# Attention values held high and low side by side: two matmuls for each value tile in place of three

## The reference

```python
kv = (rmsnorm(h_kv, kv_norm_g) @ w_ukv).reshape(B, S, MLA_HEADS, MLA_NOPE + MLA_V)   # 8 heads, 64 + 64
k_nope, v = kv[..., :MLA_NOPE], kv[..., MLA_NOPE:]
s = (jnp.einsum('bqhd,bkhd->bhqk', qn, k_nope) + jnp.einsum('bqhr,bkr->bhqk', qp, k_pe))
p = jax.nn.softmax(s.astype(jnp.float32) * scale, axis=-1).astype(v.dtype)
o = jnp.einsum('bhqk,bkhd->bqhd', p, v)
```

## Time and profile before

| what | value |
|---|---|
| median of 3 runs | 1538.49 us (1537.92 to 1539.16) |
| profiled execution, its own time | 1535.2 us |
| its span, first to last instruction | 1533.4 us |
| TensorE busy | 1472.2 us (96%) |
| VectorE busy | 780.0 us (51%) |
| ScalarE busy | 685.5 us (45%) |
| GpSimd busy | 659.9 us (43%) |
| TensorE clock granted, mean | 0.988 of full |

### The profile page before, as it was taken

One profiled execution on the slowest core, in us unless ns is written; L12 is line 12 of the kernel. 1 busy time (PEld: TensorE's weight loads), 2 busy tenths in 40 slices (PEclk: granted clock), 3 DMA queues, 4 the chain that ended last, 5 costly groups with the idle time before them and its releaser, 6 DMA issues.

```text
span 1533.4 us, 19452 instructions
## 1 busy us (share of the span) xinstructions
PE 1472.2 (96%) x6870; PEld 1201.8 (78%) x6870; DVE 780.0 (51%) x1186; ACT 685.5 (45%) x1082; POOL 659.9 (43%) x317
## 2 busy tenths in 40 slices
PE   8998899999999999999999888999999999999996
PEld 6676679888878888888878666898888888888884
DVE  7648768533464430345164776792525445014534
ACT  5556636444344431344355664463534444124432
POOL 4343226743344444343545321485443443534350
PEclk9999999999999999999999998999999999999998
DMA  5320124521233233322323101254122322422231
GB/s 199 97 82 15 42 68 139 165 83 42 83 97 107 77 118 97 96 82 82 127 83 102 50 29 55 83 169 134 41 83 82 109 82 85 124 97 84 81 96 56
DMA packets 39033, 138.76 MB, mean 90 GB/s; under 512 B 4848, under 2 KB 5104, under 8 KB 38704
## 3 DMA queue, kind: packets, MB, share of 16 engines
q1 hardware_dynamic: 37584, 134.24, 28.0%
q10 hardware_dynamic: 1376, 3.52, 0.7%
HBM read 135.64 MB, written 2.10 MB: 90 GB/s over the span
## 4 chain that ended last, share of the span: by engine, by line
PE 75%; issue 10%; DVE 8%; POOL 4%; ACT 2%; DMA 1%; SPq 0%; POOLq 0%; DVEq 0%; ACTq 0%
PE ps L1322 24%; PE ps L1324 24%; PE ps L1323 24%; POOL w_lo L340 4%; PE ps L1474 1%; DVE small L1008 1%; DMA x<-xT_d 1%; DVE h_lo L1034 0%; DVE small L1038 0%; PE ps L1497 0%; DVE arena L1034 0%; DVE work L855 0%; DVE work L1111 0%; PE ps L1332 0%; DVE work L1020 0%
## 5 line engine op out<-in xcount | busy, mean ns | idle before, releaser
L340 POOL TENSOR_TENSOR w_lo<-raw,w_hi 128x1024 fp32r<-128x1024 f32 x248 | 604.6, 2456 | 718.6 <-ACT w_hi L435 718.3
L1322 PE MATMUL ps<-h_hi,w_hi 128*128 128x512 f32 (+1 forms) x1040 | 408.2, 392 | 10.2 <-POOL w_lo L340 4.7
L1324 PE MATMUL ps<-h_hi,w_lo 128*128 128x512 f32 (+1 forms) x1040 | 404.4, 389 | 0.0
L1323 PE MATMUL ps<-h_lo,w_hi 128*128 128x512 f32 (+1 forms) x1040 | 404.1, 389 | 0.0
L435 ACT ACTIVATE w_hi<-raw 128x1024 fp32r<-128x1024 f32 x248 | 256.1, 1054 | 326.1 <-PE ps L1324 325.5
L1322 PE MATMUL ps<-arena,w_hi 128*128 128x512 f32 (+2 forms) x656 | 244.0, 372 | 0.9 <-DVE arena L990 0.9
L1324 PE MATMUL ps<-arena,w_lo 128*128 128x512 f32 (+2 forms) x656 | 242.0, 369 | 0.0
L1323 PE MATMUL ps<-arena,w_hi 128*128 128x512 f32 (+2 forms) x656 | 241.8, 369 | 0.0
L1322 PEld LDWEIGHTS ps<-h_hi,w_hi 128*128 128x128 f32 x1040 | 196.1, 189 | 53.8 <-issue 9.3
L1323 PEld LDWEIGHTS ps<-h_lo,w_hi 128*128 128x128 f32 x1040 | 196.2, 189 | 40.6 <-issue 1.0
L1324 PEld LDWEIGHTS ps<-h_hi,w_lo 128*128 128x128 f32 x1040 | 195.9, 188 | 40.5
(11 more groups left out here) (171 smaller groups left out, 1813.1 us busy)
## 6 DMA issues: line engine op xcount, KB each, us to landing
raw<-blocks_d SPq DMA_DIRECT2D x248, 512.0 KB, 3.6
x<-xT_d SPq DMA_DIRECT2D x4, 512.0 KB, 7.7
work<-memT_d ACTq DMA_DIRECT2D x2, 1024.0 KB, 5.2
outT_d<-work SPq DMA_DIRECT2D x8, 256.0 KB, 2.1
work<-ln_d ACTq DMA_DIRECT2D x2, 512.0 KB, 3.4
par<-par_d ACTq DMA_DIRECT2D x2, 113.5 KB, 5.7
work<-pos_d ACTq DMA_DIRECT2D x1, 128.0 KB, 3.7
mix_g<-par_d SPq DMA_DIRECT2D x1, 4.0 KB, 1.6
```

The costliest lines, as they stand in the source:

```text
L340: gp.tensor_tensor(w_lo[:, b % SPLIT, :], raw[:, b % RAW, :], w_hi[:, b % SPLIT, :].bitcast(F32), ALU.subtract).then_inc(lo_done.sem, 1)
L1322: pe.matmul(out, a_hi, b_hi, start=first, stop=False)
L1323: pe.matmul(out, a_hi, b_lo, start=False, stop=False)
L1324: return pe.matmul(out, a_lo, b_hi, start=False, stop=last)
```

## The change

The high and the low part of each head's values lie side by side in SBUF: 64 columns high, 64 columns low. One matmul with all 128 of them as the stationary operand gives high values by high probabilities in rows 0 to 63 of bank 5, and low values by high probabilities in rows 64 to 127. A second one, 64 wide, adds high values by low probabilities to rows 0 to 63. ScalarE copies rows 64 to 127 of the bank to SBUF (`part`, a new step at t = 2 behind `k_part`, and behind `copy_sums` for the last head). VectorE adds rows 0 to 63 to it and then multiplies by `rsum`. The value copies and subtractions write with gaps. `work` grows by one tile.

```diff
-        v_hi, v_lo = arena[:, 8:12, :], arena[:, 12:16, :]
+        v_pair = arena[:, 8:16, :].rearrange("p (k a) n -> p k (a n)", k=TT).rearrange("p k (h s d) -> p k h s d", s=2, d=VD)
+        v_hi, v_lo = v_pair[:, :, :, 0, :], v_pair[:, :, :, 1, :]
...
-        rsum = work[0:64, 11, :]
+        rsum, part = work[0:64, 11, :], work[0:64, 18, :]
...
+        part_done = sig("part_done", HEADS)
+        whole_done = sig("whole_done", HEADS)
...
-                    act.activation(v_hi[:, t, :], ps[BB[t]][:, :], ACT.Copy).then_inc(vh_done.sem, 1)
+                    act.activation(v_hi[:, t], ps[BB[t]][:, :].rearrange("p (h d) -> p h d", d=VD), ACT.Copy)\
+                        .then_inc(vh_done.sem, 1)
...
+                def copy_part(h):
+                    need(pv_mm, h + 1)
+                    if h > 0:
+                        need(o_done, h)
+                    act.activation(part, ps[5][64:128, :], ACT.Copy).then_inc(part_done.sem, 1)
...
                     if t == 2 and h + 2 < HEADS:
                         k_part(h + 2)
+                    if t == 2 and h >= 1:
+                        copy_part(h - 1)
...
                 copy_sums(HEADS - 1)
+                copy_part(HEADS - 1)
                 square_output(3)
...
                 def attended(h):
+                    need(part_done, h + 1)
+                    dve.tensor_tensor(part, ps[5][0:64, :], part, ALU.add).then_inc(whole_done.sem, 1)
+                    need(whole_done, h + 1)
                     need(rsum_done, h + 1)
-                    need(pv_mm, h + 1)
-                    dve.tensor_tensor(o_mla[64 * (h % 2):64 * (h % 2) + 64, h // 2, :], ps[5][0:64, :], rsum, ALU.mult)\
+                    dve.tensor_tensor(o_mla[64 * (h % 2):64 * (h % 2) + 64, h // 2, :], part, rsum, ALU.mult)\
                         .then_inc(o_done.sem, 1)
...
-                    c = slice(VD * h, VD * h + VD)
                     for k in ks:
-                        last = product3(ps[5][0:VD, :], v_hi[:, k, c], v_lo[:, k, c],
-                                        pt_hi[h % 2][:, k, :], pt_lo[h % 2][:, k, :], k == 0, k == TT - 1)
+                        both = v_pair[:, k, h, :, :].rearrange("p s d -> p (s d)")
+                        if k < TT - 1:
+                            pe.matmul(ps[5][:, :], both, pt_hi[h % 2][:, k, :], start=k == 0, stop=False)
+                        pe.matmul(ps[5][0:VD, :], v_hi[:, k, h, :], pt_lo[h % 2][:, k, :], start=False, stop=False)
+                        if k == TT - 1:
+                            last = pe.matmul(ps[5][:, :], both, pt_hi[h % 2][:, k, :], start=False, stop=True)
```

More of the change, by code:

```diff
@@ L128, in encoder_program @@
         arena = sb("arena", [P, 32, SEQ], F32R)
-        work = sb("work", [P, 18, SEQ])
+        work = sb("work", [P, 19, SEQ])
         turn_q = sb("turn_q", [P, 2, SEQ])
@@ L975, in layer @@
                     need(vh_done, t + 1)
-                    dve.tensor_tensor(v_lo[:, t, :],
-                                      ps[BB[t]][:, :], v_hi[:, t, :].bitcast(F32), ALU.subtract)\
+                    dve.tensor_tensor(v_lo[:, t],
+                                      ps[BB[t]][:, :].rearrange("p (h d) -> p h d", d=VD), v_hi[:, t].bitcast(F32),
+                                      ALU.subtract)\
                         .then_inc(vl_done.sem, 1)
```

## The result

The changed kernel takes 1548.45 us (median of 6 runs, 1546.04 to 1552.75); beside it the kernel before took 1538.26 (6 runs, 1534.06 to 1539.39). The ratio is 1.0077, 95% interval 1.0063 to 1.0091: slower by 10 us. The forecast was 1539.8 us, the range 1532.0 to 1546.5, so the time lies above the range.

A forecast was written before the change was run, and what follows sets the result against it. VectorE was taken to pace heads 1 and 6, TensorE or its loop through ScalarE heads 2 to 5. Per-head shifts of the sum transposes and the output projection's wait came to +1.3 us: 1539.8 us, range 1532.0 to 1546.5.

The forecast's parts named there:

- 4 matmuls less a head at 0.23 us: Each head's values product: 12 matmuls become 8, saving 0.91 us of TensorE time a head, 14.6 us in all.
- 0.73 taken: VectorE, each head: the addition ahead of the multiply adds 0.73 us, 11.7 us in all if nothing hides it.
- the multiply waiting for GpSimd: With both operands in SBUF, multiplies of heads 1, 3 and 5 meet GpSimd; each meeting costs between nothing and 2.4 us.
- the forecast column: Predicted change of each interval between sum transposes, from +0.73 at head 1 to +0.6 at the step to bank 5.
- rival 2: TensorE's clock falls after longer waits, before transposes of heads 1 (idle 3.0 us) and 5: 6 us, 1545.8; chance 0.30.
- TensorE gains 0.91 and ScalarE gives back 0.48: Head 2: shorter product less the added copy, moving the shift of the sum transposes from +0.73 to +0.3 us.
- TensorE's shorter product takes back 1.0: Head 7 and the gate: the shorter product takes off 1.0 us, the addition in the gate steps gives 0.73.
- The spare of 0.56 us: Output projection: needs bank 5 at 200.88, last multiply ended at 200.32; copy and addition delay it 1.2, TensorE waits 0.6.
- the copy's 0.48: ScalarE's added copy holds it 0.48 us a head, 7.7 us in all, leaving a gain of 0.43 in heads 2 to 5.
- six small errors: The forecast's own range of ±3 us, for steps of 0.5 us mis-sized in six places.
- Rival 3: VectorE's whole addition shows, 11.7 us, plus three meetings a layer, less TensorE's 9.1: +9, 1547.7 us; chance 0.06.
- Rival 4: A wide matmul costs as two narrow ones, so 8 matmuls cost 15 slots: +9 us again; chance 0.02.

The follow-up runs named there:

- no_sums_copy: Changed kernel without ScalarE's copy of the sums; VectorE multiplies the SBUF sum by bank 3 itself: median 1544.69 us, ratio 1.0054 to the kernel before.
- tail_order: Changed kernel with the last head's copy of the lower half ahead of the copy of its sums: ratio 1.0058 to the kernel before.
- mm_only: Changed kernel with only the shorter product: no ScalarE copy of the lower half, no VectorE addition: ratio 0.9927 to the kernel before.
- mm_copy: As mm_only with ScalarE's copy back in, VectorE waiting for it and multiplying as before, no addition: ratio 0.9986 to the kernel before.
- late_copy: Changed kernel with the copy of the lower half moved from step 2 to step 3, behind the exponential: ratio 1.0017 to the kernel before.
- sum_in_psum: Changed kernel with the sum written back to bank 5, so the multiply reads PSUM and SBUF as before: ratio 1.0070 to the kernel before.
- fillers: Changed kernel with groups of 4 spare matmuls ahead of some first scores and sum transposes, where TensorE waits: ratio 1.0074 to the kernel before.

## Why the prediction was wrong

The parts came as read: 4 matmuls less a head at 0.23 us, 0.71 for an addition and its wait (0.73 taken), and the multiply waiting for GpSimd. A forecast of +1.3 us against 9.9 comes from the sum over heads. What the sum lacked is a term for TensorE's clock: it took every matmul that is left at the speed that it had in the kernel before, and left new falls to rival 2. Of the 8.6 us that remain when the forecast column is taken from the measured one, over both layers, 5.9 are matmuls and transposes at the low clock (3.1, 2.2 and 0.6 in the first three items below). The rest is the copy, taken too small, and a gain in head 7 that TensorE did not have.

- **Head 2, 3.6 us.** The step that failed is "TensorE gains 0.91 and ScalarE gives back 0.48": the copy gave back 0.75, and the rest of the gain and more went to slower matmuls behind the longer wait. In the changed kernel TensorE waited 2.10 us for the exponential here, for 1.68 in the earlier trace rows, and the clock fell behind it. From these scores to the transposes it took 4.21 us (137.15 to 141.36), and 2.63 before. That is 1.6 us, and 1.5 in layer 1; the rest, 0.2 to 0.3 a layer, is mostly the copy. This is rival 2, at another place: it expected the fall behind head 1's transposes. There the clock was low ahead of them, from 124 to 127, at no cost, since VectorE paced; and the idle time before the transposes was 0.51 us in layer 0 and 2.10 in layer 1, not 3.0. Only in other kernels of the study, as no_sums_copy, did it fall where rival 2 had it. Timeline of TensorE in the changed kernel and the clock by stretch:

```profile
137.15 0.50 PE L1338 MATMUL ps<-arena 128*128 128x512 f32 x1 [2.10 <-ACT work L560]
138.29 1.06 PE L1490 MATMUL ps<-ident,work 128*128 128x128 f32 x4
139.58 0.63 PE L1339 MATMUL ps<-arena,w_hi 128*128 128x512 f32 x1
...
124.00:127.00 3.00, 3.00 (x10) 2.44 (x9) 2.90 (x6) 0.97 (x3) 0.00 (x0) 0.50 0.00 0
134.00:137.00 3.00, 0.89 (x6) 0.42 (x4) 3.00 (x6) 2.95 (x6) 3.00 (x3) 1.00 0.00 0
137.00:140.00 3.00, 2.85 (x9) 2.33 (x10) 2.94 (x5) 1.85 (x6) 1.37 (x1) 0.59 0.21 42
190.00:193.00 3.00, 2.88 (x11) 2.55 (x12) 2.87 (x5) 1.65 (x4) 1.75 (x1) 0.50 0.43 141
193.00:196.00 3.00, 3.00 (x11) 2.09 (x10) 0.45 (x1) 1.32 (x3) 0.00 (x0) 0.57 0.47 164
```

- **Head 7 and the last product, 3.0 us.** The step that failed is "TensorE's shorter product takes back 1.0". The first transposes of the gate, 5.71 and 5.17 us behind the sum transposes in the kernel before, split this interval. Up to there the forecast took 1.0 off; the changed kernel took 5.77 and 6.19 us, so 3.1 us of error lie in this part. The clock was low in it: in layer 0 until 195.7, 5.5 us from the transposes on, where before it had come back after 3.3. tail_order has the same instructions there, and in its layer 0, where the clock came back sooner, the part took 4.88 us: the low clock made up about 0.9 and 1.3 us. The other 0.9 is the forecast's: layer 1 of the kernel before ran this part at the high clock in 5.17 us, TensorE waiting for VectorE, and even mm_only, without copy and addition, needed 4.70 in both layers. The gate steps behind it took 0.73 us more, as forecast, and the last product 0.7 and 2.0 us less, for 0.9 and 1.7. The part by kernel, layer 0 then layer 1: before, changed, mm_only, and layer 0 of tail_order:

```profile
183.30:189.01 5.71, 5.71 (x24) 4.19 (x25) 3.75 (x4) 2.97 (x6) 2.27 (x1) 0.71 0.50 172
932.15:937.32 5.17, 4.31 (x24) 2.91 (x25) 3.78 (x4) 2.85 (x6) 2.30 (x1) 1.00 0.56 180
190.12:195.89 5.77, 5.76 (x20) 4.53 (x21) 3.20 (x4) 2.96 (x6) 1.63 (x1) 0.53 0.46 153
943.93:950.12 6.19, 6.10 (x20) 4.41 (x21) 4.22 (x4) 3.26 (x7) 2.37 (x1) 0.52 0.39 131
183.44:188.14 4.70, 3.39 (x20) 2.49 (x21) 3.77 (x4) 2.45 (x6) 2.29 (x1) 1.00 0.49 154
926.62:931.32 4.70, 3.42 (x20) 2.49 (x21) 3.76 (x4) 2.46 (x6) 2.28 (x1) 1.00 0.45 148
191.72:196.60 4.88, 4.88 (x20) 3.65 (x21) 3.94 (x4) 2.60 (x7) 2.36 (x1) 0.65 0.41 130
```

- **To bank 5, 1.1 us.** The spare of 0.56 us was read rightly; the delay was 0.61 for the copy and 0.72 for the addition. A last low-clock stretch added 0.3 us a layer at the transposes. tail_order took 2.0 us of 2.3 away by turning two lines round.
- **Head 4, 0.5 us; heads 3 and 6, 0.4.** The term that was taken too small is the copy's 0.48: it costs the loop 0.75 us by the rows under mm_copy, and 0.7 to 0.8 by the head (head 2 of layer 1: 11.66 in mm_copy, 10.86 in mm_only). So heads 2 to 4 of mm_copy, where they had no fall, gained 0.1 to 0.3 us against before, not 0.43. I had taken the spacing of a copy on the row of another copy; this one starts later behind its forerunner.

The forecast's own range of 3 us was meant for six small errors that would partly cancel. They did not: what was added took turns on the path, the falls came on top, and nearly every mistake was of one sign. mm_only, mm_copy and the changed kernel make the chain plain: stretches of 220.2, 230.2 and 240.9 us for 231.0 before. The matmuls give 10.7, the copy takes 10.0, the addition 10.6. The copy's 10.0 hold two falls (head 2 in layer 0, head 3 in layer 1; 2.9 us) and late_copy shows that 6.9 us of the changed kernel's loss hang on the copy's place. The addition's 10.6 are near 16 x 0.71 = 11.4 only by chance: they hold a meeting of 1.16 us a layer, head 3 of layer 1 lost its fall, and for heads 1, 3 and 5 the multiply of the kernel before already started 0.70 to 0.72 us behind its forerunner (0.59 to 0.60 for heads 0, 2, 4 and 6), so that the addition made 0.6 us there, not 0.73.

Rival 2, at 0.30, had the mechanism of most of the miss and nearly its size (6 us), at other places. Its reading of the waits was too narrow: it went by the waits of 1.65 and 1.74 us behind which the clock was low, and passed over the same two waits in the other layer, behind which it was high (below). Rival 3, at 0.06, had nearly the total, +9, but by luck: it had every addition shown in full beside three meetings a layer and no fall, and of the meetings only that of head 3's multiply is shown to cost time (1.16 us, by sum_in_psum). Rival 4 has a slip in its sum: four wide matmuls at double cost and four narrow ones are 12 slots, as before, not 15. The trace rules it out in any case, as matmuls of the changed product still start 0.23 us apart.

**Open.** Why the clock falls at one wait and not at its twin: after 2.09 us in mm_copy it fell in layer 0 and not in layer 1. The kernel before shows the same. These two transposes, behind waits of 1.66 and 1.74 us, came at the high clock (0.65 us); in the earlier trace rows those of the same heads in the other layer, behind 1.65 and 1.74 us, came at the low one (1.12 and 1.11 us):

```profile
172.13 0.65 PE L1497 MATMUL ps<-ident,small 128*128 128x128 f32 x4 [1.66 <-DVE small L1014]
932.15 0.65 PE L1497 MATMUL ps<-ident,small 128*128 128x128 f32 x4 [1.74 <-DVE small L1014]
```

Nor does the length of a single wait decide it: in layer 0 of the changed kernel the clock fell at 124, behind waits of 1.09 and 0.69 us. The runs show what a fall cost, not what brings it.

## What to carry to other kernels

Where three engines hand work round a loop by turns, an engine's idle time in a window is no cover for added work: before counting an instruction as hidden, find who waits for what stands behind it in its queue. Put a new step behind the one that others wait for (6.9 us here for one moved copy), and pay for a shorter matmul chain only in the stretches where TensorE is the one waited for (worth 1.8 us here by the medians, and hardly clear of the noise). Where a change lengthens TensorE's waits, give the clock a term in the sum (in these kernels a fall cost up to 1.6 us where TensorE was on the path), and look up the same wait in every repetition in the trace before saying where the clock will fall.

## What was not expected of the hardware

- ScalarE's copy from rows 64 to 127 of a bank starts 0.61 to 0.62 us behind its forerunner. The copy of the sums, from rows 0 to 63 of another bank, with two waits of its own as well, starts 0.49 us behind the same kind of forerunner (line 568 in both cases). Behind the new copy, an instruction that reads a bank from row 0 again also starts 0.61 to 0.62 us later (the exponential in head 5, line 568 in late_copy), and one that reads SBUF 0.49 to 0.50; where two of the latter lie between, the exponential behind them is the one that is 0.13 us late (the rows under mm_copy). The change of the first row may be the cause; it was not tried alone.
- Spare matmuls in a wait can keep the clock up there and let it fall at the next wait (fillers: 1.5 us less in head 2, 2.5 more in head 3). Waits of equal length in one program had either outcome, in the kernel before too.
- An addition that reads and writes the same PSUM bank kept its spacing (head 1 took 13.87 us with the sum in SBUF and 13.89 with it in PSUM), and kept the multiply clear of GpSimd.
